# Block products for the attention projections of a hybrid retention and attention layer, with two copies moved from DVE to ACT

## What is computed

```
h = rms_norm(x);  p = h @ w_in           # 2048 x 7168
retention (8 heads of 128: q, k, v, gate) and chunked attention (8 heads: q, k, v)
attention: q, k -> rms_norm over 128; scores + relative bias, mask, softmax; @ v
retention: rotary q, k; (q @ k.T) * decay; @ v; group norm; * silu(gate)
x = x + concat(ret, att) @ w_out
x = x + square(relu(rms_norm(x) @ w_ff1)) @ w_ff2
```

## Time and profile before

| | before |
|---|---|
| median of 3 runs | 1105.76 us |
| the profiled execution | 1104.85 us, of it span 1103.1 us |
| TensorE clock | 1.000 in the whole span |
| PE, PEld busy | 1097.7 us, 932.3 us |
| DVE, ACT busy | 857.8 us, 695.4 us |
| POOL busy | 53.4 us |
| DMA | 263.81 MB, mean 239 GB/s |

### The profile page before, as it was taken

One profiled execution on the slowest core, in us unless ns is written; L12 is line 12 of the kernel. 1 busy time (PEld: TensorE's weight loads), 2 busy tenths in 40 slices (PEclk: granted clock), 3 DMA queues, 4 the chain that ended last, 5 costly groups with the idle time before them and its releaser, 6 DMA issues.

```text
span 1103.1 us, 13129 instructions
## 1 busy us (share of the span) xinstructions
PE 1097.7 (100%) x5190; PEld 932.3 (85%) x5190; DVE 857.8 (78%) x803; ACT 695.4 (63%) x827; POOL 53.4 (5%) x69
## 2 busy tenths in 40 slices
PE   9999999999999999999999999999999999999998
PEld 9789989989988888888888888888888888888887
DVE  7876876866866678869778879778869787869784
ACT  6964664674674555777655677655677655577662
POOL 0100100100100000000000000000000000000000
DMA  9975774775776647878788787797787787787792
GB/s 360 306 255 173 206 254 170 198 263 173 191 277 217 242 178 198 263 264 239 226 297 229 252 282 218 233 299 221 254 284 214 243 290 222 261 277 221 245 279 93
DMA packets 43965, 263.81 MB, mean 239 GB/s; under 512 B 4864, under 2 KB 7680, under 8 KB 16256
## 3 DMA queue, kind: packets, MB, share of 16 engines
q1 hardware_dynamic: 37712, 220.61, 53.7%
q0 software_dynamic: 5760, 41.95, 20.3%
q10 hardware_dynamic: 432, 0.41, 0.1%
HBM read 260.85 MB, written 2.10 MB: 238 GB/s over the span
## 4 chain that ended last, share of the span: by engine, by line
PE 95%; ACT 0%; DVE 0%; issue 0%; DVEq 0%
PE acc L931 10%; PE acc L927 10%; PE acc L929 10%; PE acc L797 7%; PE acc L810 7%; PE acc L804 7%; PE bankC L889 4%; PE acc L889 4%; PE bankC L882 4%; PE acc L882 4%; PE acc L884 4%; PE bankC L884 4%; PE acc L624 2%; PE acc L629 2%; PE acc L636 2%; PE bankD L889 1%
## 5 line engine op out<-in xcount | busy, mean ns | idle before, releaser
L1779 DVE TENSOR_TENSOR w_lo<-raw,w_hi 128x2048 fp32r<-128x2048 f32 x180 | 410.8, 2288 | 126.8 <-ACT w_hi L1300 126.5
L1300 ACT ACTIVATE w_hi<-raw 128x2048 fp32r<-128x2048 f32 x180 | 344.7, 1916 | 220.0 <-PE acc L931 146.6
L1497 DVE TENSOR_TENSOR w_lo<-raw,w_hi 128x1024 fp32r<-128x1024 f32 (+1 forms) x150 | 164.9, 1110 | 47.5 <-ACT w_hi L1053 47.4
L1053 ACT ACTIVATE w_hi<-raw 128x1024 fp32r<-128x1024 f32 (+1 forms) x150 | 140.6, 965 | 21.6 <-DVE raw L1506 12.6
L797 PE MATMUL acc<-w_hi,hT_hi 128*128 128x384 f32 (+1 forms) x408 | 104.3, 374 | 0.1
L927 PE MATMUL acc<-w_hi,hF_hi 128*128 128x512 f32 x256 | 100.8, 394 | 0.0
L931 PE MATMUL acc<-w_hi,hF_lo 128*128 128x512 f32 x256 | 99.7, 390 | 0.0
L929 PE MATMUL acc<-w_lo,hF_hi 128*128 128x512 f32 x256 | 99.6, 389 | 0.0
L804 PE MATMUL acc<-w_hi,hT_lo 128*128 128x384 f32 (+1 forms) x408 | 97.7, 357 | 0.0
L810 PE MATMUL acc<-w_lo,hT_hi 128*128 128x384 f32 (+1 forms) x408 | 97.2, 356 | 0.0
L927 PE MATMUL acc<-w_hi,dF_hi 128*128 128x512 f32 x248 | 96.9, 391 | 0.0
(11 more groups left out here) (276 smaller groups left out, 1798.9 us busy)
## 6 DMA issues: line engine op xcount, KB each, us to landing
raw<-in_w_up SPq DMA_DIRECT2D x64, 1024.0 KB, 6.5
raw<-in_w_down SPq DMA_DIRECT2D x64, 1024.0 KB, 6.5
raw<-in_w_ret SPq DMA_DIRECT2D x32, 1024.0 KB, 5.7
raw<-in_w_att SPq DMA_DIRECT2D x28, 768.0 KB, 4.5
raw<-in_w_out SPq DMA_DIRECT2D x16, 1024.0 KB, 4.8
raw<-in_w_up POOLq DMA_DIRECT2D x16, 1024.0 KB, 8.8
raw<-in_w_down POOLq DMA_DIRECT2D x16, 1024.0 KB, 9.1
raw<-in_w_ret POOLq DMA_DIRECT2D x8, 1024.0 KB, 9.0
```

The costliest lines, as they stand in the source:

```text
L1053: nc.scalar.activation(piece(w_hi, q, 0, n), raw[:, r, half * n:(half + 1) * n], ACT.Copy).then_inc(hi_done, 1)
L1300: nc.scalar.activation(w_hi[:, ring(s)], raw[:, r, :], ACT.Copy).then_inc(slab_hi, 1)
L1497: nc.vector.tensor_tensor(piece(w_lo, q, 0, n), raw[:, IN_PLAN[i, READ_AT.get(step, step)][0], half * n:(half + 1) * n], piece(w_hi, q, 0, ...
L1779: nc.vector.tensor_tensor(w_lo[:, ring(s)], raw[:, r, :], w_hi[:, ring(s)].bitcast(f32), ALU.subtract).then_inc(slab_lo, 1)
```

## The change

Blocks 1 to 3 compute their two attention heads as a block product too: the upper half of the weights by seven steps of 384 columns (q1, p5, p6, p7, p3, q2, p4), 12 matmuls each, the lower half by I2, I3, J2, J3. The first block stays ordinary for attention. The retention steps Z1, Q2, Z2, P4, H1, H2 of a block move behind its P3, among the attention steps of the next. A "pair" n is now an attention pair (n odd) or a retention pair (n even); sums, kept results and bank settings are made for each. Where a step starts a bank anew (`fresh`), only block 0 still computes 512 columns. `att_norm` of heads 2 to 7 and the copy of the retention keys are ACT's, `att_norm` of heads 0 and 1 stays with DVE. All tables of turns are new, and a few buffers and counts follow (`first_of`, `ring`, `a_proj_first`). Positions (turns, pieces) count from the first piece of the block's new order, where Z1 is 0 and 1; those over 43 lie in the next block. Of the tables below the first is PE's, the second ACT's and the third DVE's.

```diff
...
-STEPS = ["I0 J0 I1 J1 I2 Q1 J2 P5 I3 P6 J3 P7 P3 Z1 Q2 Z2 P4 H1 H2".split()] + [
-    "I0 I1 I2 I3 J0 Q1 J1 P5 J2 P6 J3 P7 P3 Z1 Q2 Z2 P4 H1 H2".split()] * (BLOCKS - 1)
-LOADS = ["I0 J0 I1 J1 I2 a J2 b I3 d J3 Z1 e Z2 H1 H2".split()] + [
-    "I0 I1 I2 I3 J0 a b J1 J2 d J3 Z1 e Z2 H1 H2".split()] * (BLOCKS - 1)
-LEAD = LOADS[0][:SLABS]
+IN_ORDER = [(0, step) for step in "I0 J0 I1 J1 I2 Q1 J2 P5 I3 P6 J3 P7 P3".split()]
+IN_LOADS = [(0, name) for name in "I0 J0 I1 J1 I2 a J2 b I3 d J3".split()]
+IN_STARTS = [0]
+for _i in range(1, BLOCKS + 1):
+    _r, _here = "Z1 Q2 Z2 P4 H1 H2", "Z1 Q2 q1 Z2 P4 p5 H1 p6 H2 p7 p3 I2 q2 Q1 I3 p4 P5 J2 P6 J3 P7 P3"
+    _loads = "Z1 e A Z2 B D H1 H2 I2 E a I3 b d J2 J3" if _i < BLOCKS else "Z1 e Z2 H1 H2"
+    IN_STARTS.append(2 * len(IN_ORDER))
+    _before = ["Z1", "Q2", "Z2", "P4", "H1", "H2", "e"]
+    IN_ORDER += [(_i - (step in _before), step) for step in (_here if _i < BLOCKS else _r).split()]
+    IN_LOADS += [(_i - (name in _before), name) for name in _loads.split()]
+IN_NO = {block_step: s for s, block_step in enumerate(IN_ORDER)}
+LEAD = IN_LOADS[:SLABS]
...
 def ret_banks(u):
-    return (bankA, bankB) if u % 2 else (bankC, bankD)
+    return (bankC, bankD) if u == HEADS - 2 else (bankA, bankB)
...
+quarter = {"a": (0, 0), "b": (1, 0), "e": (0, 1), "d": (1, 1)}
 if name[0] in "IJ":
     row, table, n = ((2 * i + (name[0] == "J")) * SLABS + int(name[1])) * P, w_att, N_ATT
+elif name in quarter:
+    row, table, n = pair_row(2 * i, *quarter[name]), w_ret, N_RET
+elif name.lower() in quarter:
+    row, table, n = pair_row(2 * i - 1, *quarter[name.lower()]), w_att, N_ATT
 else:
-    c, k = {"a": (0, 0), "b": (1, 0), "e": (0, 1), "d": (1, 1), "Z1": (1, 2), "Z2": (1, 3),
-            "H1": (0, 2), "H2": (0, 3)}[name]
-    row, table, n = ((2 * i + c) * SLABS + k) * P, w_ret, N_RET
+    row, table, n = pair_row(2 * i, int(name[0] == "Z"), 1 + int(name[1])), w_ret, N_RET
...
+for i in range(1, BLOCKS):
+    add_b(2 * i - 1)
+    add_e(2 * i - 1)
+    ret_power(2 * i - 2)
+    mask_bias(i)
+    add_b(2 * i)
+    ret_power(2 * i - 1)
+    att_power(2 * i)
+    add_e(2 * i)
     att_power(2 * i + 1)
...
+n, up = in_pair(i, step), step.upper()
+if up == "Q1" and n:
+    pe.wait_ge(y_set, n)
+    pe.wait_ge(w_set, n)
+elif up == "P5":
     pe.wait_ge(sf_lo_ok, 1)
-    if i:
-        pe.wait_ge(p5_kept, i)
-elif step == "P6":
+    if n:
+        pe.wait_ge(p5_kept, n)
+elif up == "P6":
     pe.wait_ge(sf_lo_ok, 2)
-    pe.wait_ge(q1_kept, i + 1)
-elif step == "P7":
+    pe.wait_ge(q1_kept, n + 1)
+elif up == "P7":
     pe.wait_ge(sf_lo_ok, 3)
-    pe.wait_ge(z_set, i + 1)
-elif step == "P3":
+    pe.wait_ge(z_set, n + 1)
+elif up == "P3":
     pe.wait_ge(sf_lo_ok, 4)
-elif step == "Z1" and m == 1:
-    pe.wait_ge(w_set, i + 1)
-elif step == "Q2":
-    pe.wait_ge(h_set, i + 1)
-elif step == "P4":
-    pe.wait_ge(y_set, i + 1)
+elif (up == "Z1" or up == "I2" and i) and m == 1:
+    pe.wait_ge(w_set, n + 1)
+elif up == "Q2":
+    pe.wait_ge(h_set, n + 1)
+elif up == "P4":
+    pe.wait_ge(y_set, n + 1)
...
-fresh = step in ("I0", "J0", "Q1", "P5") and t == 0
-wide = N if fresh else n
+fresh = step.upper() in ("I0", "J0", "Q1", "P5") and t == 0
+wide = N if fresh and i == 0 else n
...
+for h in range(HEADS):
+    i, second = h // 2, h % 2
+    places = ((23, 25, 27, 28), (29, 31, 34, 36))[second] if i == 0 else (
+        (35, 37, 41, 43), (46, 48, 51, 53))[second]
+    for pos, f in zip(places, (att_T, att_scores, att_PT, att_pv)):
+        at_piece(i, pos, f, h)
+for u in range(HEADS):
+    i, second = u // 2 + 1, u % 2
+    places = ((12, 13, 16, 20), (23, 25, 27, 31))[second] if i < BLOCKS else (
+        (9, 10, 11, 13), (13, 14, 15, 17))[second]
+    for pos, f in zip(places, (ret_T, ret_scores, ret_y, ret_ZT)):
+        at_piece(i, pos, f, u)
...
+def att_norm(h):
+    act.wait_ge(a_rs_ok, h + 1)
+    act.wait_ge(a_mix_lo, h)
+    if h % 2 == 0:
+        act.wait_ge(r_mix_lo, h)
+    for m in range(MT):
+        for s in range(2):
+            i = 2 * m + s
+            ins = nc.scalar.activation(a_qk[:, m, s * HD:(s + 1) * HD], att_rows(h)[:, m, s * HD:(s + 1) * HD],
+                                       ACT.Copy, scale=a_rs[:, i:i + 1])
+    ins.then_inc(a_qk_ok, 1)
...
 def ret_qT(u):
     act.wait_ge(r_T, u + 1)
     nc.scalar.activation(r_qT[:], ret_banks(u)[0][:, 0:SEQ], ACT.Copy).then_inc(r_qT_ok, 1)
+    nc.scalar.activation(r_kT[:], ret_banks(u)[1][:, 0:SEQ], ACT.Copy).then_inc(r_kT_ok, 1)
...
+for i in range(1, BLOCKS):
+    h, u, n = 2 * i, 2 * i - 2, 2 * i
+    at_piece(i, 6, keep_in_q1, n - 1)
+    at_piece(i, 8, ret_proj, u)
+    at_piece(i, 9, ret_tanh, u)
+    at_piece(i, 12, keep_in_p5, n - 1)
+    at_piece(i, 13, ret_qT, u)
+    at_piece(i, 18, ret_proj, u + 1)
+    at_piece(i, 19, ret_scale, u)
+    at_piece(i, 20, set_y, n - 1)
+    at_piece(i, 21, set_h, n - 1)
+    at_piece(i, 21, ret_mix, u)
+    at_piece(i, 21, ret_tanh, u + 1)
+    at_piece(i, 24, ret_qT, u + 1)
+    at_piece(i, 28, keep_in_q1, n)
+    at_piece(i, 30, ret_scale, u + 1)
+    at_piece(i, 30, att_proj, h)
+    at_piece(i, 31, att_squares, h)
+    at_piece(i, 32, ret_mix, u + 1)
+    at_piece(i, 34, keep_in_p5, n)
+    at_piece(i, 34, att_norm, h)
+    at_piece(i, 36, att_qT, h)
+    at_piece(i, 39, att_exp, h)
+    at_piece(i, 40, att_proj, h + 1)
+    at_piece(i, 41, att_squares, h + 1)
+    at_piece(i, 42, att_pT, h)
+    at_piece(i, 42, set_y, n)
+    at_piece(i, 43, set_h, n)
+    at_piece(i, 44, att_mix, h)
+    at_piece(i, 45, att_norm, h + 1)
+    at_piece(i, 47, att_qT, h + 1)
+    at_piece(i, 49, att_exp, h + 1)
+    at_piece(i, 52, att_pT, h + 1)
+    at_piece(i, 54, att_mix, h + 1)
...
+def in_sum(n, other, read):
+    r, o, cols = pair_raw(n, "a")[0], pair_raw(n, other), slice(0, SLAB_KT * pair_cols(n))
     dve.wait_ge(in_raw[o[0]], o[1])
-    dve.wait_ge(lo_done, in_first(i, read) + 2)
-    nc.vector.tensor_tensor(raw[:, r, :], raw[:, r, :], raw[:, o[0], :], ALU.add).then_inc(in_summed, 1)
-def set_z(i):
-    dve.wait_ge(p5_kept, i + 1)
-    dve.wait_ge(piece_used, in_first(i, "P6") + 2)
-    dve.wait_ge(acc_read_act, 8 * i + 1)
-    nc.vector.tensor_tensor(bZ[:], in_p5[:], bX[:], ALU.subtract).then_inc(z_set, 1)
-def set_w(i):
-    dve.wait_ge(piece_used, in_first(i, "P7") + 2)
-    dve.wait_ge(acc_read_act, 8 * i + 2)
-    nc.vector.tensor_tensor(bW[:], in_p5[:], bX[:], ALU.subtract).then_inc(w_set, 1)
+    dve.wait_ge(lo_done, pair_first(n, read) + 2)
+    nc.vector.tensor_tensor(raw[:, r, cols], raw[:, r, cols], raw[:, o[0], cols],
+                            ALU.add).then_inc(in_summed, 1)
...
-def ret_kT(u):
-    dve.wait_ge(r_T, u + 1)
-    nc.vector.tensor_copy(r_kT[:], ret_banks(u)[1][:, 0:SEQ]).then_inc(r_kT_ok, 1)
...
+for i in range(1, BLOCKS):
+    h, u, n = 2 * i, 2 * i - 2, 2 * i
+    at_piece(i, 3, in_sum, n - 1, "b", "Q1")
+    at_piece(i, 9, ret_rotate, u)
+    at_piece(i, 11, ret_rotated, u)
+    at_piece(i, 11, in_sum, n - 1, "d", "P5")
+    at_piece(i, 14, ret_decay, u)
+    at_piece(i, 16, set_z, n - 1)
+    at_piece(i, 17, ret_norm, u)
+    at_piece(i, 19, set_w, n - 1)
+    at_piece(i, 20, ret_rotate, u + 1)
+    at_piece(i, 21, ret_mix, u)
+    at_piece(i, 21, ret_rotated, u + 1)
+    at_piece(i, 26, ret_decay, u + 1)
+    at_piece(i, 26, in_sum, n, "b", "Q1")
+    at_piece(i, 28, ret_norm, u + 1)
+    at_piece(i, 31, in_sum, n, "d", "P5")
+    at_piece(i, 32, ret_mix, u + 1)
+    at_piece(i, 32, att_mean_squares, h)
+    at_piece(i, 38, set_z, n)
+    at_piece(i, 38, att_bias_max, h)
+    at_piece(i, 40, att_probs, h)
+    at_piece(i, 41, set_w, n)
+    at_piece(i, 42, att_mean_squares, h + 1)
+    at_piece(i, 44, att_mix, h)
+    at_piece(i, 49, att_bias_max, h + 1)
+    at_piece(i, 50, att_probs, h + 1)
+    at_piece(i, 54, att_mix, h + 1)
...
```

More of the change, by code:

```diff
@@ L508, in _ @@
             load_decay(1)
[L509 to L519, removed]
+            for i, name in IN_LOADS[11:]:
+                load_in(i, name)
+                if name == "D":
+                    load_bias(i)
+                elif name == "J3":
+                    load_decay(2 * i)
+                    load_decay(2 * i + 1)
             load_group(G_OUT, w_out, 0, N)
@@ L565, in ret_power, with add_second @@
                 nc.gpsimd.tensor_tensor(r_rs[:], r_ve[:], neg_half[:, 0:MT], ALU.pow).then_inc(r_rs_ok, 1)
-            def add_ret(i, into, c, k, done, count):
-                row = ((2 * i + c) * SLABS + k) * P
-                nc.gpsimd.dma_start(raw[:, IN_PLAN[i, into][0], :], w_ret[row:row + P, :],
+            def add_second(n, into, c, done):
+                table, cols = w_att if n % 2 else w_ret, SLAB_KT * pair_cols(n)
+                row = pair_row(n, c, 1)
+                nc.gpsimd.dma_start(raw[:, pair_raw(n, into)[0], 0:cols], table[row:row + P, :],
@@ L571, in add_ret, with add_b @@
                                     accum_op=ALU.add).then_inc(done, 16)
```

(48 more changed lines are left out.)

334 lines of the change are left out of this document (139 added, 195 removed).

## The result

The changed kernel takes 1114.8 us (median of 5 runs, 1112.47 to 1117.34) against 1105.76 us, a ratio of 1.0085 with a 95% interval of 1.0062 to 1.0107. The forecast was 1100.8 us with a range to 1104.8. The profiled execution took 1117.34 us, its span is 1115.5 us, and it is the longest of the five.

What follows compares the result with a forecast made beforehand. PE was taken as the bound, 95% of the chain. A 6.8 us saving less 1.9 us of added waits gave 4.9 us less, so a median of 1100.8 us, with a range of 1098.5 to 1104.8.

Steps and rivals of the forecast that it cites:

- The saving on PE: Blocks 1 to 3: 12 fewer matmuls each, 6.2 us, plus 0.5 us from narrower bank starts at I0 and J0.
- The prices of the added work: Per block DVE gets a net 8.1 us, to 69.1 us, and ACT 10.8 us, to 61.4, of 81.3 us.
- Step (a): Raw buffers from I3 to J2 and H1 to Z2: 4.8 us of PE time; holds only through DVE's lead, 2.7 to 4.2.
- rival 1: Late raw slabs at H1 (1.1 us) and J2 (0.3 us) eat the saving, 5 us in all, giving 1104; chance 0.13.
- The sign named for a fault in (a): ACT waiting for DMA before H1 or J2 would show the raw-buffer step wrong.
- POOL's queue: Waits in turn for add_b, add_e, two powers of retention, add_b, the powers of attention; landings hidden.
- It costs nothing: Key copy on ACT behind the query copy, 0.38 us later, covered by a piece of 1.37 us or more.
- Nothing again: Small scalings between ACT's hi pieces delay what follows by 1.6 us; two prepared pieces cover 2.1 us or more.
- Step (b): DVE from p7 to P5: 25.1 us against PE's 24.8; the lead covers it, about 1 us spare at J2.
- rival 2: DVE becomes the bound of a block, PE waiting for w_lo at I3 to J2: kernel at 1113; chance 0.11.
- The sum: PE's extra waiting set at 0.65 us in each of three blocks, 1.9 us, leaving 4.9 us saved.
- ceiling of 6.8 us: The most the change can save on PE, if PE waits no more than before.

Runs made afterwards that it cites:

- kernel 9: Kernel 7 with DVE's second retention sum at turn 33 instead of 31 and ACT's scaling of the first attention head at 33 instead of 34: 1102.2 us, 0.9968.
- 1: The changed kernel with POOL's accumulating DMA of a retention pair held until J2 landed, the wait also ahead of the second retention head's power: 1117.4 us, 1.0105.
- 11: The changed kernel with POOL's accumulating DMA of the retention pair held until J2 landed, the second head's power made first, DVE's sums unmoved: 1106.0 us, 1.0004.
- 10: The kernel before the change with only the copy of the retention keys moved to ACT, the scaling left to DVE: 1105.6 us, 1.0001.
- 6: Kernel 5 with ACT's copies of a block's first retention queries and keys in turn 11 instead of 13, ahead of p6's copy: 1103.15 us, 0.9976.
- 3: The changed kernel with both moves to ACT undone, att_norm of heads 2 to 7 and the retention key copy on DVE again: 1114.2 us, 1.0074.
- 4: The kernel before the change with the two moves to ACT alone, its order of steps and products untouched: 1108.3 us, 1.0026.
- 12: Kernel 9 with the scaling of attention heads 2 to 7 back on DVE, only the key copy staying with ACT: 1104.35 us, 0.9989.
- 5: The changed kernel with DVE's first sum of a retention pair one turn later, 27 in place of 26: 1106.4 us, 1.0005.
- 7: Kernel 6 with POOL making the second retention head's power first and holding the retention pair's accumulating DMA until J2 landed: 1102.9 us, 0.9975.
- 8: The kernel before the change with PE made to wait ahead of J2 in blocks 1 to 3 for six POOL clears: 1118.3 us, 1.0116.

## Why the prediction was wrong, point by point

**The saving on PE** held: 36 matmuls, and blocks of the mended kernel with PE near full.

**The prices of the added work** held. The sum of 1536 elements took 1754 ns (1.76 us in the prediction), the bank settings on DVE 555 ns and on ACT 475 ns, the small scalings 392 ns. In these lines of the changed kernel, 89 to 340 us, as the earlier trace rows:

```profile
L1581 DVE TENSOR_TENSOR raw<-raw 128x1536 f32<-128x1536 f32 x4 | 7.0, 1754 | 0.2
...
L1597 DVE TENSOR_TENSOR acc<-in_p,bankC 128x384 f32<-128x384 f32 x3 | 1.7, 555 | 0.0
```

```profile
L1143 ACT ACTIVATE a_qk<-a_proj,a_rs 128x128 f32<-128x128 f32 x12 | 3.9, 392 | 1.4 <-DVE zT_lo L1680 1.4
```

DVE and ACT are busy 69.7 and 61.1 us of the stretch of the earlier trace rows in kernel 9, 83.6 us and so a little over a block, against 69.1 and 61.4 forecast.

**Step (a), where it is tight: the raw buffers, failed.** The place and the partner were right (J2 takes I3's buffer, 4.8 us of PE time between), and rival 1 named it. Its size was wrong: 0.3 us at J2, and 3.4 us were measured. The term that failed is the landing of 4.5 us. That is the median of all attention loads before; at this place it was 10.6, 9.8 and 9.9 us. The overlap that was left out is the one with POOL's accumulating DMA: the prediction has the sum at turn 26, POOL's 1 MB behind it and I3 as the one that frees J2's buffer, each by itself. The sum stands just before the low part of I3's second piece, so the DMA and J2's load go out 0.6 us apart. With the DMA held back (1, 11) the load landed in 4.1 to 5.5 us, under the 6.7 that it had, and the wait was gone. The lead that (a) relied on held, if barely: DVE freed I3's buffer 2.7 us before PE was through with I3, the lower end of the 2.7 to 4.2 us. The sum had taken 2.2 us of that lead, which the walk through (a) leaves out, because (a) was reckoned in PE time and (b) in DVE time. The larger term of rival 1, 1.1 us at H1, did not come: H1's loads landed in 7.0 to 7.4 us and PE did not wait. The sign named for a fault in (a), ACT waiting for DMA before J2, is what the trace shows.

POOL's queue was read wrongly too: the power of the second retention head stands behind the second `add_b`, not ahead of it. In the change this cost nothing that the waits show, but the edit of 1 ran into it.

**The clock** stood in no term. All rivals priced a wait at its own length. In the change a wait at J2 cost 1.8 us more on average by the balance, and 2.3 us by the pace of the weight loads.

**"It costs nothing" for the key copy** was right for the copy (10) and wrong for the place. The row that served as cover, ACT idle before that copy, was of the old order. In the new one ACT stands up to 4.7 us before p6's high part, behind DVE's sum, so both copies came late, 1.2 us a block; 6 won back 3.2 us. It was the queue position that cost; at the turns tried, the copy on DVE's side came later still (3).

**"Nothing again" for the scaling** was wrong in the old order, 2.7 us by 4 and 10. Whether it was in the changed order can't be read off the change; 12 says it is worth 2.2 us there. In the old order the lead of two pieces did not cover it, as PE's new waits at P5 show (4); what had used the lead up was not followed. The price of a small scaling was right, 0.392 us against 0.394; what failed is that PE would not wait for them.

**Step (b), DVE's full stretch,** was right in kind and place: PE's wait for w_lo of J2 behind the second sum, 1.0 us a block in 5, 6, 7. "About 1 us to spare" was 2 us too much. As rival 2 had it, the cause of a slower kernel, it is refuted by 5: 8.4 us went by moving one sum, with DVE's load unchanged. That rival 2's time, 1113, lies near the measured 1114.8 is luck.

**The sum** let PE's wait double, 1.9 us more in three blocks. The late slab apart, that term was too small as well: in 11, where no load is late, the other waits of PE's weight loads from 60 to 360 us sum to 9.8 us against 2.0 before, 7.8 more. That takes the whole ceiling of 6.8 us, and 11 takes 1106.0 us. The late copies before `ret_scores` are 3.6 us of it, the low part behind the second sum 3.0 and the scaled queries 2.4.

Of the ceiling of 6.8 us the best order keeps 3.3 to 3.6 us (1102.2 against 1105.5 measured beside it and 1105.76 at first, ratio 0.9968). The rest are PE's waits: 5.7 us in the three blocks by the rows of 9, where it waited 2.0 before.

## What to carry to other kernels

A load that takes over a buffer must be timed as one chain: the last reader's place in its engine's queue, the issue, and the landing beside what the same event releases on the other queues; a median of landings is not its price. In in-order queues a task costs by where it stands, not by its length: one turn of one sum, which also turned round the order of a load and a 1 MB DMA, was worth 8.4 us, and two turns of a pair of copies 3.2 us. A move between engines has to be tried anew when the order of work changes, as its sign can turn.

## What was not expected of the hardware

- The granted clock fell to 0.50 for about 5 us of PE's work after a PE wait of 3.9 us that followed 30 us of full work. With three equal gaps of 3.4 us it fell in two blocks and stayed at 1.00 in one (8); it fell behind a wait of 2.9 us and stayed at 1.00 behind one of 3.0 (3). The five runs of the change spread over 5 us with mean clocks of 0.992 to 0.998; those of the later kernels without such a wait over 1.6 us at most. But the four runs of 1, with a wait of 3.8 us and clocks of 0.995 to 0.998, lie within 0.3 us.
- A 768 KB load issued 0.6 us after an accumulating DMA of 1 MB landed in 9.8 to 10.6 us, in 4.1 to 5.5 us with that DMA held back (1, 11), and in 4.1 to 4.2 us when it went out 2.5 us ahead of it (5); in block 1 of the change the share of the DMA engines was 1.02 and 0.98 in the ten microseconds between.
- A PE gap of 3.4 us was not made up by the work that ACT and DVE had ready: 10.1 us of gaps, with 3.1 us of half clock behind two of them, made the kernel 12.6 us longer.
